# Attention heads carried inside the gate slabs of a two-block layer stack

## The reference, cut to what matters

```python
x = x + 0.5 * swiglu(rmsnorm(x, ffn1_norm), ffn1_w_gu, ffn1_w_down)
h = rmsnorm(x, mix_norm);  z = h @ w_in            # u, v, c_q, c_kv, k_rope, q_m, gates
y_a = spatial_gating(gelu(u), gelu(v), ...)        # layer norm of v, mix over 128 tokens, times u
y_b = mla(c_q, c_kv, k_rope, ...)                  # latent norms, 8 heads of 96, rope, causal softmax
y_c = memory_attention(q_m, mem, ...)              # 4 heads of 128 over 256 memory tokens, k and v from rmsnorm(mem)
gates = sigmoid(z[..., COL_GATE:] + b_gate)        # 3 x 1024
merged = gates[0] * (y_a @ w_branch_a) + gates[1] * (y_b @ w_branch_b) + gates[2] * (y_c @ w_branch_c)
x = x + merged @ w_out
x = x + 0.5 * swiglu(rmsnorm(x, ffn2_norm), ffn2_w_gu, ffn2_w_down)
```

## Time and profile before

| | us |
|---|---|
| median of three runs | 1976.53 |
| lowest, highest | 1973.66, 1989.18 |
| the profiled execution | 1977.42 |
| its span | 1975.7 |
| PE busy | 1736.5 |
| DVE busy | 1059.7 |
| ACT busy | 845.9 |
| POOL busy | 273.7 |

### The profile page before, as it was taken

The page is one execution under the profiler, slowest core; times in us unless marked ns, Lnnn a source line. Parts: engine busy times, 40 slices in busy tenths (PEclk is TensorE's granted clock), DMA queues, the critical chain, the costliest instruction groups (busy, mean ns, idle before and its releaser), DMA issues.

```text
span 1975.7 us, 32472 instructions
## 1 busy us (share of the span) xinstructions
PE 1736.5 (88%) x13057; PEld 1632.8 (83%) x13057; DVE 1059.7 (54%) x1327; ACT 845.9 (43%) x1253; POOL 273.7 (14%) x335
## 2 busy tenths in 40 slices
PE   6986898888989997986789997999898977788998
PEld 5975888878979996974689997999898835588998
DVE  5852755537368845434468835444446443455444
ACT  5651233244456634441456534344445513343332
POOL 0000444400013310000013300220000000011210
PEclk8995899998989998986799998999899977798999
DMA  5440111024425442530235444555554321153544
GB/s 211 170 148 15 46 45 45 1 96 163 149 91 182 148 153 97 215 127 0 97 106 171 139 162 147 193 178 179 186 187 146 111 86 54 65 188 131 191 161 137
DMA packets 41565, 252.81 MB, mean 128 GB/s; under 512 B 4524, under 2 KB 6688, under 8 KB 19472
## 3 DMA queue, kind: packets, MB, share of 16 engines
q1 hardware_dynamic: 37376, 233.13, 34.7%
q0 software_dynamic: 4112, 18.61, 3.1%
HBM read 250.55 MB, written 1.17 MB: 127 GB/s over the span
## 4 chain that ended last, share of the span: by engine, by line
PE 78%; DVE 13%; ACT 5%; issue 2%; DMA 1%; POOL 0%; DVEq 0%; SPq 0%; ACTq 0%; POOLq 0%
PE bank L378 20%; PE bank L379 20%; PE bank L380 19%; DVE w_lo L272 2%; PE bank L382 2%; PE bank L516 2%; PE bank L1041 2%; ACT w_hi L269 2%; PE bank L1049 1%; PE bank L1052 1%; DVE a L478 1%; DVE rs L472 1%; PE bank L465 1%; PE bank L1804 1%; PE bank L1428 1%
## 5 line engine op out<-in xcount | busy, mean ns | idle before, releaser
L378 PE MATMUL bank<-work_r,w_hi 128*128 128x272 f32 (+1 forms) x3376 | 971.4, 288 | 68.1 <-DVE work_r L417 58.0
L379 PE MATMUL bank<-work_r,w_hi 128*128 128x272 f32 (+1 forms) x3376 | 967.3, 287 | 0.0
L380 PE MATMUL bank<-work_r,w_lo 128*128 128x272 f32 (+1 forms) x3376 | 964.5, 286 | 0.0
L272 DVE TENSOR_TENSOR w_lo<-ring,w_hi 128x2048 fp32r<-128x2048 f32 (+2 forms) x233 | 487.3, 2093 | 546.0 <-ACT w_hi L269 546.0
L378 PEld LDWEIGHTS bank<-work_r,w_hi 128*128 128x128 f32 x3376 | 647.4, 192 | 73.6 <-issue 56.7
L269 ACT ACTIVATE w_hi<-ring 128x2048 fp32r<-128x2048 f32 (+2 forms) x233 | 408.7, 1755 | 565.8 <-PE bank L380 565.5
L379 PEld LDWEIGHTS bank<-work_r,w_hi 128*128 128x128 f32 x3376 | 647.1, 192 | 0.1
L380 PEld LDWEIGHTS bank<-work_r,w_lo 128*128 128x128 f32 x3376 | 646.7, 192 | 0.0
L1201 DVE SCALAR_TENSOR_TENSOR work<-work,params_sb 128x272 f32<-128x272 f32 x176 | 122.5, 735 | 5.9
L1211 POOL TENSOR_TENSOR work<-work 128x272 f32<-128x272 f32 x44 | 44.9, 1021 | 353.9 <-ACT work L1185 353.9
L465 PE MATMUL bank<-sq,consts_sb 128*128 128x272 f32 (+1 forms) x202 | 59.2, 452 | 32.7 <-ACT sq L446 22.3
(11 more groups left out here) (369 smaller groups left out, 1761.6 us busy)
## 6 DMA issues: line engine op xcount, KB each, us to landing
ring<-in_stream SPq DMA_DIRECT2D x166, 1024.0 KB, 4.9
ring<-in_stream SPq DMA_DIRECT2D x64, 704.0 KB, 4.1
ring<-in_stream SPq DMA_DIRECT2D x10, 768.0 KB, 4.3
work<-rows_scratch POOLq DMA_DIRECT2D x4, 1632.0 KB, 8.0
work<-rows_scratch POOLq DMA_DIRECT2D x4, 544.0 KB, 9.0
work<-rows_scratch_o POOLq DMA_DIRECT2D x1, 2176.0 KB, 9.6
ring<-in_stream SPq DMA_DIRECT2D x3, 512.0 KB, 3.6
work<-rows_scratch_m POOLq DMA_DIRECT2D x1, 1088.0 KB, 7.0
```

Of the source, the lines that this page charges most:

```text
L272: eng.tensor_tensor(w_lo[:, slot, 0:size], raw_w, w_hi[:, slot, 0:size].bitcast(F32), ALU.subtract).then_inc(lo_done, 1)
L378: pe.matmul(out, w_hi[:, slot, at:at + P], hi, start=first, stop=False)
L379: pe.matmul(out, w_hi[:, slot, at:at + P], lo, start=False, stop=False)
L380: mm = pe.matmul(out, w_lo[:, slot, at:at + P], hi, start=False, stop=last)
```

## The change

The phases are put in another order: `mem_k` first, then `in_uv`, `in_cq_kr`, `in_ckv`, `in_qm`, `mla_q`, `mla_k`, `mla_v`, `mem_v`, and `in_gates` last, just ahead of `branches`. (The layout of the stream in memory stays; `STORED` keeps it.)

The squares of memory are made on POOL, its sums come on PE between `up2` and `down2`, and its norm on DVE at the start of `down2`. The memory keys are then multiplied right behind the sums of the norm ahead of the mixers. Spatial gating, the latent norms and the head norms are spread over the small projections. The square root's table is loaded fewer times (`table=False`).

The twelve heads become one list, and head j stands at the start of gate slab j: PE does the scores of head j, the transposes of head j-1 and the values of head j-2, and then the slab. `scores_pe`, `turn_pe`, `values_pe`, `softmax_dve`, `exp_act`, `turn_act` and `values_act` hold the same instructions as `attention` did. Gates leave PSUM with their bias alone, and the sigmoid is applied later by `gate_curve`, in five instructions.

In the diff below the unchanged bodies are left out.

```diff
@@ -56,12 +57,18 @@
     ("ml_gates", 1, 1, 1, 8, False), ("ml_in", 12, 2, 1, 16, True), ("ml_out", 4, 2, 1, 16, True),
     ("up1", 22, 2, 1, 16, True), ("down1", 16, 1, 2, 11, True),
     ("up2", 22, 2, 1, 16, True), ("down2", 16, 1, 2, 11, True),
-    ("in_uv", 4, 2, 1, 16, True), ("in_cq_kr", 2, 2, 1, 16, True), ("in_qm", 2, 2, 1, 16, True), ("in_ckv", 1, 2, 1, 16, True),
-    ("in_gates", 12, 2, 1, 16, True), ("mla_q", 2, 4, 1, 12, False), ("mla_k", 1, 8, 1, 16, False), ("mla_v", 1, 2, 1, 8, False),
-    ("mem_k", 2, 2, 1, 16, False), ("mem_v", 2, 2, 1, 16, False),
+    ("mem_k", 2, 2, 1, 16, False),
+    ("in_uv", 4, 2, 1, 16, True), ("in_cq_kr", 2, 2, 1, 16, True), ("in_ckv", 1, 2, 1, 16, True), ("in_qm", 2, 2, 1, 16, True),
+    ("mla_q", 2, 4, 1, 12, False), ("mla_k", 1, 8, 1, 16, False), ("mla_v", 1, 2, 1, 8, False), ("mem_v", 2, 2, 1, 16, False),
+    ("in_gates", 12, 2, 1, 16, True),
     ("branches", 8, 3, 1, 12, True), ("mix_out", 4, 2, 1, 16, True),
     ("up3", 22, 2, 1, 16, True), ("down3", 16, 1, 2, 11, True),
 ]
...
@@ -1401,11 +1415,15 @@
         def mem_pool(pool):
             pool.wait_ge(*S.at("norm_add", 7, 3))
             pool.dma_start(memn, mem_t.rearrange("(k p) t -> p k t", p=P)).then_inc(S.sem("mem_in"), 16)
-        def mem_squares(act):
-            act.wait_ge(S.sem("mem_in"), 16)
+            pool.wait_ge(S.sem("mem_in"), 16)
             for k in range(DB):
-                square(act, k, memn[:, k, :], SEQ, "mem")
+                S.inc(pool.tensor_tensor(mem_sq0[:, k, :], memn[:, k, :], memn[:, k, :], ALU.mult), "mem_squares", k)
+        def mem_norm_pe(pe):
+            for k in range(DB):
+                pe.wait_ge(*S.at("mem_squares", k))
+                mm = pe.matmul(stat["mem"][:, 0:SEQ], ones, mem_sq0[:, k, :], start=(k == 0), stop=(k == DB - 1))
+            S.inc(mm, "mem_pe", "sums")
...
+        def rope_turn_dve(dve, i):
             inc = lambda ins, step=None: S.inc(ins, "mla_dve", step)
-            own = lambda: S.own(dve, "mla_dve")
+            both = lambda v: v.unsqueeze(1).broadcast_to([QK, 2, SEQ])
+            x = qk16[0:QK, 2 * i:2 * i + 2, :]
+            tmp = turned[i % 2][0:QK]
+            if i == 0:
...
+            inc(dve.tensor_tensor(tmp, ps[(7, 4)[i % 2]][0:QK, :].rearrange("p (a b) -> p a b", b=SEQ), both(trig[0:QK, 2, :]), ALU.mult), f"rope{i}")
+            inc(dve.tensor_tensor(x, x, both(trig[0:QK, 3, :]), ALU.mult))
+            S.own(dve, "mla_dve")
+            inc(dve.tensor_tensor(x, x, tmp, ALU.add))
+        def heads_dve(dve):
             dve.wait_ge(S.sem("mla_rows_in"), 32)
-            dve.wait_ge(*S.at("rope_act"))
-            both = lambda v: v.unsqueeze(1).broadcast_to([QK, 2, SEQ])
-            for i in range(8):
+            S.own(dve, "mla_dve")
+            for i in (0, 4, 1, 5, 2, 6, 3, 7):
                 x = qk16[0:QK, 2 * i:2 * i + 2, :]
-                tmp = prob[i % 2][0:QK, :].rearrange("p (a b) -> p a b", b=SEQ)
-                dve.wait_ge(*S.at("mla_pe", f"rot{i}"))
-                inc(dve.tensor_tensor(tmp, ps[4 + i % 2][0:QK, :].rearrange("p (a b) -> p a b", b=SEQ), both(trig[0:QK, 2, :]), ALU.mult), f"rope{i}")
-                inc(dve.tensor_tensor(x, x, both(trig[0:QK, 3, :]), ALU.mult))
-                own()
-                inc(dve.tensor_tensor(x, x, tmp, ALU.add))
-                own()
-                if i == 3:
-                    rown_dve(dve, 4, SEQ, 8)
-                inc(dve.tensor_tensor(x, x, (sq_q if i < 4 else sq_k)[0:QK, 2 * i % 8:2 * i % 8 + 2, :], ALU.mult), "heads" if i == 7 else None)
-            own()
+                S.inc(dve.tensor_tensor(x, x, (sq_q if i < 4 else sq_k)[0:QK, 2 * i % 8:2 * i % 8 + 2, :], ALU.mult), "mla_dve",
+                      "heads" if i == 7 else None)
...
-        def memq_pool(pool):
-            pool.wait_ge(*S.at("rown_dve", "rows", 4))
-            pool.wait_ge(*S.at("mla_dve", "heads"))
+        def mem_rows_pool(pool):
+            pool.wait_ge(*S.at("rown_dve", "rows", 3))
             pool.dma_start(scr_c, rrow[0:8, 0, 0:SEQ]).then_inc(S.sem("mem_rows_out"), 16)
             pool.wait_ge(S.sem("mem_rows_out"), 16)
-            pool.dma_start(sq_q, on_all(scr_c, 0, (SEQ, 8), (1, SEQ))).then_inc(S.sem("mem_rows_in"), 16)
...
+        def gates_pe(pe, x):
+            def between(j):
+                scores_pe(pe, j)
+                if j >= 1:
+                    turn_pe(pe, j - 1)
+                if j >= 2:
+                    values_pe(pe, j - 2)
+            stream_pe(pe, "in_gates", x, SEQ, between=between)
+            turn_pe(pe, HEADS - 1)
+            values_pe(pe, HEADS - 2)
+            values_pe(pe, HEADS - 1)
+        def gate_curve(act, m, lo, hi):
+            S.inc(act.activation(gat[:, m, lo:hi, :], gat[:, m, lo:hi, :], ACT.Sigmoid), "gate_act", f"gate{m}.{hi}")
+        def gates_act(act):
+            def between(j):
+                if j >= 1:
+                    turn_act(act, j - 1)
+                if j >= 2:
+                    values_act(act, j - 2)
+                exp_act(act, j)
+                if j == 9:
+                    split_branch_act(act, 0)
+                if j == 11:
+                    act.preload_act_table(ACT.Sigmoid)
+                    act.wait_ge(*S.at("att_act", "o7"))
+                    split_branch_act(act, 1)
+                    phase_read(act, "in_gates", 22)
+                    gate_curve(act, 0, 0, 8)
+            def body(un):
+                un.ready(act)
+                if un.j == 0:
+                    act.wait_ge(*S.at("memq_dve"))
+                un.free(act.activation(gat[:, un.j // DB, un.j % DB, :], un.bank()[:, 0:SEQ], ACT.Identity, bias=pm("b_gate", un.j)))
+            each_product(act, "in_gates", 1, body, split="hi", between=between)
+            turn_act(act, HEADS - 1)
+            values_act(act, HEADS - 2)
+            values_act(act, HEADS - 1)
+            act.wait_ge(*S.at("att_act", f"o{HEADS - 1}"))
+            split_branch_act(act, 2)
+            phase_read(act, "in_gates")
+            for half in range(2):
+                for m in (1, 2):
+                    gate_curve(act, m, 4 * half, 4 * half + 4)
+        def gates_dve(dve):
+            def between(j):
+                softmax_dve(dve, j)
+                if j == 9:
+                    split_branch_dve(dve, 0)
+            each_product(dve, "in_gates", 1, nothing, split="lo", between=between)
+            split_branch_dve(dve, 1)
+            split_branch_dve(dve, 2)
...
@@ -2017,24 +2053,46 @@
             norm_act(act, 8, H2, 8, SEQ, D, ready=lambda k: act.wait_ge(*S.at("norm_add", k, 3)))
             split_act(act, 7, a, A2_HI, 8, SEQ, ready=normed(act, 8))
             up_act(act, "up2")
+            norm_act(act, 0, None, 8, SEQ, D, kind="mem")
             residual_squares(act, "down2", "hi")
-            norm_act(act, 9, None, 8, SEQ, D)
+            norm_act(act, 9, None, 8, SEQ, D, table=False)
             split_act(act, 8, a, A2_HI, 8, SEQ, ready=normed(act, 9))
-            in_act(act)
+            mem_k_act(act)
+            project(act, "in_uv", ACT.Gelu, lambda j: (uT if j < 4 else vT)[:, j % 4, :])
+            act.preload_act_table(ACT.Sin)
             rope_act(act)
-            mla_in_act(act)
-            rown_act(act, 3, [], SEQ, 16, 1.0 / QK, cn("eps"))
-            mem_k_act(act)
+            act.preload_act_table(ACT.Sqrt)
+            project(act, "in_cq_kr", ACT.Copy, lambda j: cqT[:, j, :])
+            phase_read(act, "in_cq_kr")
+            for k in range(3):
+                square(act, k, cqT[:, k, :], SEQ, "cq")
+            sg_squares_act(act)
+            project(act, "in_ckv", ACT.Copy, lambda j: ckvT[:, j, :])
+            phase_read(act, "in_ckv")
+            for k in range(2):
+                square(act, k, ckvT[:, k, :], SEQ, "ckv")
+            norm_act(act, 0, None, 3, SEQ, 384, kind="cq", table=False)
+            sg_root_act(act)
+            def qm_act(un):
+                if un.j == 2:
+                    norm_act(act, 0, None, 2, SEQ, 256, kind="ckv", table=False)
+                un.ready(act)
+                un.free(act.activation(qmT[:, un.j, :], un.bank()[:, 0:SEQ], ACT.Copy))
+            each_product(act, "in_qm", 1, qm_act, turns=0, split="hi")
+            phase_read(act, "in_qm")
             phase_read(act, "mem_k")
-            memq_act(act)
-            attention(act, "act", "mla")
-            prepare(act, "hi", "branches")
-            act.wait_ge(*S.at("mlaatt_act", "o7"))
-            split_branch_act(act, 0)
-            split_branch_act(act, 1)
-            attention(act, "act", "mem")
-            act.wait_ge(*S.at("mematt_act", "o3"))
-            split_branch_act(act, 2)
+            rown_squares(act, [(qmT, mem_sq[:, 0:4, :]), (kmem, mem_sq[:, 4:8, :])])
+            mla_q_act(act)
+            sg_tok_act(act)
+            rown_act(act, 3, [], SEQ, 8, 1.0 / P, cn("eps"), table=False)
+            mla_k_act(act)
```

(87 more changed lines are left out.)

520 lines of the change are left out of this document (243 added, 277 removed).

## The result

The kernel with the change takes **1923.28 us**, the median of four runs (1915.32 to 1924.02); the kernel before took 1979.14 us on the same chip (four runs, 1973.66 to 1989.18). The ratio is 0.9725, with a 95% interval of 0.9693 to 0.9758. The forecast was 1924 us. The profiled execution took 1922.57 us, with a span of 1920.9 us against 1975.7. In a later session the same kernel was run again, and one of its six runs, 4295.03 us, is left out of the ratio given there.

What follows compares the result with a forecast made beforehand. PE bounds the kernel, with idle and slow time in the heads that gate slabs could cover. 305.9 - 247.3 - 3.45 - 0.7 - 0.7 = 53.8 us off 1977.4 gives 1924 us; range 1907 to 1950.

Steps and rivals of the forecast that it cites:

- Steps 1 and 2: Norm ahead of the mixers: mem_k covers it, so in_uv starts at 14.0 us and its four slabs end at 35.8.
- Step 3: Before in_ckv: PE waits 3.65 us for w_lo behind the rope angles, and the slow clock costs 1.75 us more.
- Steps 4 to 6: Latent norms to sums of 16 heads: PE waits 4.15 us on the mixing, 1.7 more in clock; sums start at 111.1.
- Step 7: Before the gate slabs: DVE's head scalings end at 141.5 us; PE waits 6.1 us and pays 2.65 for its clock.
- Step 8: Twelve gate slabs with the heads: PE sets the pace, 65.3 us plus 24.7 for heads, last slab ending at 237.9.
- the first rival: Gate slabs: the softmax chain of up to 9.1 us, not PE, sets them; 12 us longer, 1936 us; chance 0.18.
- Step 9: Tail from the last gate slab to the third part of branches: 9.4 us, ending at 247.3.
- Outside the stretch: Outside norm sums' end to third part of first branches slab: added costs of 3.45, 0.7 and 0.7 us.
- One sign of being wrong: First feed-forward of the second block: the prediction fails if it grows by more than 5 us.
- run cold: Small projections: the clock stays at half through t=96 to 142; 1934 us; chance 0.12.
- POOL's transfers were not held back: Head rows' transfers: POOL can't issue until DVE pauses, so heads start near 149; 1932 us; chance 0.05.
- The slower rival: Gate slabs: stops at each head lower the clock to half, 7.5 us more a slab; 2014 us; chance 0.04.

Runs made afterwards that it cites:

- keys' experiment: The changed kernel with mem_k put back behind in_qm, so nothing covers the norm ahead of the mixers: 1929.06 us, ratio 0.9758.
- loads on DVE: The changed kernel with one extra DVE operation of 1.22 us, or of 0.42 us, ahead of each head's softmax: 1923.93 us and 1919.65 us.
- the second: Second profile of the changed kernel, from running it again unaltered: 1922.05 us, ratio 0.9708.
- the first experiment: The changed kernel with the twelve heads taken out of the gate slabs and run behind them: 1969.07 us, ratio 0.9982.

## Why the prediction was right, step by step

**Steps 1 and 2** hold: `in_uv` starts at t=13.8 (forecast 14.0) and its last product is out at 35.7 (35.8). Of the table load that the prediction counts into the 6.6 us of before, only the last 0.5 us lies in them. The keys' experiment shows the cover: 10.1 us longer without it.

**Step 3** holds: the angles are done at 45.3 (45.4), `w_lo` for `in_ckv` at 51.8 (52.05), the wait is 3.5 us (3.65), the clock 0.60 for the 3.4 us behind it, and the latent sums start at 59.2 (59.3). ACT in order of time in the changed kernel:

```profile
1462.08 0.63 ACT L1664 ACTIVATE a<-a 96x512 f32<-96x512 f32 x1 [6.12 <-DVE a L1659]
1462.73 1.28 ACT L2064 ACT_TABLE_LOAD   x1
1464.02 0.38 ACT L1532 ACTIVATE work<-bank 128x256 f32<-128x256 f32 x1
```

The load ends at 1464.01 and the next instruction starts at 1464.02. Nothing of a drain shows, so the rule in the Trainium skill, ScalarE: Activation LUTs, What ACT_TABLE_LOAD costs, that adds about 1.38 us to every switch, is not borne out by this trace. The prediction's 2.8 us by that rule was also twice what it could give here: the first of the two loads lies beside DVE's angles, and ACT still stands 6.12 us behind it, so one switch alone is on the chain.

**Steps 4 to 6** hold to 0.1 us until the mixing: first rotation at 96.1 (96.0), first addition done at 102.9 (102.9), PE's wait 4.1 (4.15). Then **one term was too small**: the clock's price behind it, 1.7 forecast, 3.4 measured (0.50 for 4.8 us and 0.78 for 4.5 more). The sums of 16 heads start at 112.9 (111.1). Taking the wait away gave 7.3 us, which is 4.1 and about this price.

**Step 7** holds: the head scalings end at 142.7 (141.5) and the wait is 5.3 us (6.1). DVE is 1.2 us later, PE 2 us.

**Step 8, the heart of it,** was right in kind: PE sets the slabs, 7.44 us apart at a clock of 1.00. The last gate slab ends at 233.8 (237.9) despite the later start, so 5.3 us of the forecast were too much. The hand-offs, for which I chose 0.3 us a slab, cost nothing: 3.6 us. Most of the rest is the memory heads, set at four thirds of a causal one, 2.7 us, which took 2.2 to 2.3. Both terms were choices and not readings. The loads on DVE show that the chain of the first rival is real and has only some half a microsecond to spare. Its 12 us did not come.

**Step 9** holds: one wait of 3.5 us on ACT's copy, behind the table load, split and sigmoid. From the end of the last gate slab to the third part of `branches` it is 10.2 us (9.4). The forecast's own mark is the start of this part on PE, 1660.84 us in the changed kernel: 244.05 us from the start, forecast 247.3.

**Outside the stretch** one term holds (3.45 for memory's sums, measured 3.6), and two are smaller (0.7 for the late weights of `in_uv`, measured 0.1; 0.7 for the first `w_hi` of `branches`, where all that stands behind the stretch grew by 0.3). **Two were not foreseen**, and together cancel what the stretch gained over its forecast: 6.8 us lost to the pace of `up2` and `down2`, and 3.4 us won ahead of them in unchanged code. The total is so close, 1923.28 to 1924, partly by luck: the forecast of the stretch, on its own mark, was 58.6 us of gain and it gave 62.0.

**One sign of being wrong did show.** The prediction said that it fails if the first feed-forward of the second block (`up2` and `down2`) grows by more than 5 us. In the first profile it grew by 6.8 us without memory's sums, in the second by 2.2, where `up2` had its faster pace. What the sign was to catch, a cost that the change puts on the feed-forward, is at most the 2.3 us of `down2`; the rest comes and goes between executions of one kernel.

**The other rivals.** The small projections did not run cold as a whole; in the first profile the clock fell behind each of the three waits and came back. The head rows' long transfer, with DVE busy throughout, was quicker than before:

```profile
sq<-rows_scratch_q POOLq DMA_DIRECT2D x1, 1024.0 KB, 6.8
```

So POOL's transfers were not held back. DVE's work there is float32 additions, products, a reciprocal and `w_lo`. Whether any of these is an operation of the kind that the rule of the Trainium skill, SBUF — State Buffer, SBUF: two separate sides, speaks of, no run here shows. The slower rival needed a stop at each head long enough to lower the clock, and found 0.4 us in all. What such stops do the first experiment shows: there PE stands 2.15 and 0.64 us in each head's turn of 6.81 us, and the clock is 0.50 from 1630 to 1677 us. That the change does nothing is what the first experiment looks like, 1969.07 us against the 1967 of that rival: heads that cost their own time.

## What to carry to other kernels

A chain of short steps round three engines (here 6.8 us a head by itself, for 2.0 us of PE at its full clock) belongs between slabs that keep PE streaming, spread out so that each step has a slab's time. Before doing it, add up the chain and hold it against the slab, since here half a microsecond decided. Then look at each wait of over 3 us that is left. In the first profile there are four in this stretch, and each cost itself and 1.7 to 3.4 us of low clock behind it. Three of them went by moving work of DVE and ACT that nobody waited for yet out from in front of work that PE waited for. Compare two profiles by stretches between marks and not by spans alone, since unchanged code can differ by several microseconds between executions.
